# Rebuilding the attention slot of a two-layer encoder kernel: transposes move into the score banks, and ScalarE alone empties them

## Chip, cores and metric

One Trainium2 chip, one core. The metric is the device time in microseconds of one execution of the whole program, which is one launch. Smaller is better.

## What is computed

One inference step of a two-layer streaming encoder, in float32, for 1024 prompt frames and 64 sample frames (1088 columns in all, `TOK`), with 256 cached frames for the sample stream. Each layer is

```python
x = x + rmsnorm(mixer(rmsnorm(x)))
x = x + rmsnorm(squared_relu_mlp(rmsnorm(x)))
```

The mixer of layer 0 has two kinds of heads, and layer 1 has a third:

```python
# kind A, 4 heads with two maps each (differential attention, chunk-causal, ALiBi)
w = softmax(s0 + bias) - lam * softmax(s1 + bias);  oa = rmsnorm(w @ v)
# kind B, 8 heads: softmax(s + decay) @ v, causal, decay = cum_q - cum_k
# kind C, 16 heads: softmax(s + table[clip(q - k)]) @ v over the own chunk and 8 chunks before
```

Queries, keys and values come from one product of the normed input with `w_in`, and new keys and values are outputs too.

## The kernel before

**Layout.** Everything is kept feature-major: 128 features on the partitions, the 1088 columns along the free axis, in the chunks 384, 384 and 320 (`CHUNKS`). Float32 products are made as three f32r products (high x high, low x high, high x low), so one 128x128 weight tile times one chunk is three matmuls, and one *step* (one chunk of one of Q, K and V, 8 weight tiles) is 24 matmuls, called products here (`product`, L1175, the matmul at L1180). Weights arrive as units of 128x1024: SyncE loads one into `WS`, ScalarE casts it to `WH` (`hi_unit`, L647, L653), GpSimd subtracts for `WL` (`lo_unit`, L519, L522).

**Attention groups.** 16 groups of 128 features, each with two heads (or the two maps of kind A), run one after the other: 4 of kind A, 4 of B, 8 of C. While the attention of group g runs, TensorE also makes the Q, K and V of group g+1 in 9 steps (216 products), which keep it busy between the attention matmuls. The last group of each layer has no such products (`proj=False`, "alone" below). An iteration is one group; it is a hardware loop on every engine (`runs`, L370).

**Slots.** An iteration has 11 slots. The queries are taken in blocks of 128 in the order 7, 6, 5, 4, 3, 2, 1, the sample block, 0 (`ORDER`). In slot s TensorE makes the scores of block number s (`scores`, L1223: Q high/low times K high/low, 6 matmuls for each head and bank, heads side by side on the two halves of the array). VectorE adds the bias and takes the maximum (`scores`, L981, the operation at L988, which writes `PR`, and L993), ScalarE takes the exponential (`exps`, L748, L752), VectorE divides by the sum (`sums`, L1024, L1032, or the combination at L1038 for kind A). Then the probabilities are transposed on TensorE (L1271) 128 columns at a time, copied out of PSUM to `PT`, and multiplied with the transposed values `V` (L1286, L1290) to give the output of the block, which VectorE copies to `OT` (L1016); for kind A it is normed first and transposed back (L1019 to L1058, L1274, L740). Kind B and C have two heads to transpose, kind A one combined map. A block has up to 1024 keys in kinds A and B and up to 640 in C.

**PSUM.** 8 banks of 512 columns. Banks 0 and 1 hold the products in turn, 2 to 5 the scores (two for each head), 6 and 7 everything else. `bank_uses` (L77) lists what passes through banks 6 and 7 in an iteration: values, transposes in pieces of up to four tiles, the output, the output's transpose. The pieces take the two banks in turn, and each waits until the piece two before it is emptied (`use_bank`, L1251, semaphores `xA` and `xD`). Pieces are emptied by ScalarE and VectorE in turn, in practice one engine for each bank (`empty`, L732 and L1003).

**Order by hand.** Slots 0 to 7 have one step of products each, the ninth step is spread over slots 8 to 10 (`SLOT_PRODUCTS`). `S_AT` says after how many products of a slot the scores come (24, that is all of them, in slot 0; 0 from slot 3 on), `T_AT` where the transposes of the block before come. The output of a block follows at the end of the slot in which it is transposed.

**Between iterations.** At the top of an iteration ScalarE casts `Qh` and `Kh` (L769, L771) once all 9 steps are emptied, VectorE subtracts for `Ql` and `Kl` (L1062, L1064), and `scores(0)` on TensorE waits for `qklo`. SyncE loads the bias tables for the group at the top of its iteration, and stores K, V and the output.

Of the kernel before, what the change touches and what calls it, by code (L numbers as in the profile page):

```python
# [20 lines left out]
P = 128  # L21
D_MODEL, D_FF = 1024, 4096
KT_D = D_MODEL // P
# [11 lines left out]
S_AT = {k: [24, 8, 4, 0, 0, 0, 0, 0, 0] for k in "ABC"}  # L35
S_AT["alone"] = [0] + [12] * 8

T_AT = {k: [(12, 22)] * 8 + [(2, 6), (9, 13), (14, 24)] for k in "ABC"}
T_AT["alone"] = [(1, 11)] * 11

SLOT_PRODUCTS = [(0, 3 * KT_D)] * 8 + [(0, 6), (6, 14), (14, 3 * KT_D)]
# [26 lines left out]


class Use:  # L70


    def __init__(self, what, block, m, tiles, engine):
        self.what, self.block, self.m, self.tiles, self.engine = what, block, m, tiles, engine


def bank_uses(kind):  # L77

    slots = [[] for _ in range(11)]
    for n, t in enumerate(([0, 1, 2], [3, 4, 5, 6], [7, SAMPLE + 2])):  # L80
        slots[0].append(Use("V", None, 0, t, "AD"[n % 2]))
    for s in range(1, 11):
        ot = [Use("OT", ORDER[s - 2], 0, [], "A")] if s >= 2 and kind == "A" else []
        if s == 10:
            slots[s] += ot
        else:
            b = ORDER[s - 1]
            tiles = key_tiles(kind, b)
            n = 0
            for m in range(1 if kind == "A" else 2):  # L90
                for o in range(0, len(tiles), 4):
                    slots[s].append(Use("T", b, m, tiles[o:o + 4], "AD"[n % 2]))
                    n += 1
            slots[s] += ot + [Use("PV", b, 0, tiles, "D")]
    flat = [u for slot in slots for u in slot]
    count = {"A": 0, "D": 0}
    for n, u in enumerate(flat):
        u.n = n
        count[u.engine] += 1
        u.nth = count[u.engine]  # L100
        u.bank = n % 2
        u.prev = flat[n - 2] if n >= 2 else None
    return slots, flat, count


USES = {k: bank_uses(k) for k in "ABC"}
# [45 lines left out]
FROM_ONE = ("S", "ttr", "xpe", "xA", "xD")  # L152


def make_sections():
# [4 lines left out]
    def attention(layer, kind, g0, reps, proj):  # L160
        _, flat, count = USES[kind]
        per = dict(qkhi=2, qklo=2, S=18, ttr=18, nm=18, ex=18, ri=9, xpe=len(flat), xA=count["A"], xD=count["D"],
                   bias=16 if kind == "A" else 32, vc=16, kst=16, vst=16, evD=9 * proj)
        if kind == "A":
            per.update(cs=9, comb=9, ms=9, rs=9, on2=9)
        else:
            per.update(sc=18)
# [93 lines left out]
def build_program(nc, x_in, w_in, gains_in, subg_in, bf_in, lam_in, kcache, vcache, logf_cache, alibi, rel_bias,  # L261
# [4 lines left out]
    with ctx:  # L266
# [54 lines left out]
        ON, a = place("ON", a, [P, P])  # L321
# [21 lines left out]
        def semaphore(name):  # L343
# [7 lines left out]
                 "xpe xA xD "  # L351
                 "ms rs on2 "
# [43 lines left out]
        def transposed(use, bank):  # L396

            rows = [P if use.what == "V" and t != SAMPLE + 2 else N_SAMPLE if use.what == "V" else t[1] for t in use.tiles]
            first = use.tiles[0] if use.what == "V" else use.tiles[0][0] // P
            buf = V[:, :, :] if use.what == "V" else PT[:, use.m, :, :]  # L400
            full = sum(n == P for n in rows)
            out = []
            if full:
                out.append((buf[:, first:first + full, :].rearrange("p t q -> p (t q)"), bank[:, 0:full * P]))
            if full < len(rows):
                last = use.tiles[-1] if use.what == "V" else first + full
                out.append((buf[0:N_SAMPLE, last, :], bank[0:N_SAMPLE, full * P:(full + 1) * P]))
            return out


        @block.sync
        def _(sp):
# [9 lines left out]

# [14 lines left out]
            for sec in SECTIONS:  # L437
# [16 lines left out]
                elif sec.kind == "ATT":  # L454
                    if sec.g0 % GROUPS == 0:
                        norms_over(sp, sec)
                        sp.wait_ge(sem["toep"], 16)
# [1003 lines left out]
```

## Time and profile before

| | |
|---|---|
| median of 3 runs | 3188.15 us (3185.65 to 3194.68) |
| profiled execution, own time | 3186.88 us |
| its span, first to last instruction | 3185.1 us |
| TensorE busy in the span | 2909.5 us (91%) |
| VectorE, ScalarE, GpSimd busy | 1473.7, 841.5, 660.7 us |
| mean granted TensorE clock | 0.954 of full speed |
| one iteration with products, kinds A, B, C | about 75.4, 79.0, 71.8 us |
| the two groups alone, last product before to first product after | 78.1 and 75.1 us |

A row of the trace with the line L1180 is a product. "Idle before" is what an engine stood still just before an instruction, with what ended it. Matmuls are pipelined: the time from one start to the next is what a matmul costs, the duration behind it is longer.

### The profile page before, as it was taken

The page shows a single profiled execution, that of the slowest core. Times are in us where ns is not written, and L with a number is a line of the kernel's source. Part 1 is how long each engine was busy: PE and PEld are TensorE (multiplying, and loading weights), DVE is VectorE, ACT ScalarE, POOL GpSimd, SP SyncE. Part 2 cuts the span into 40 slices and gives each one's busy share as a digit, 9 for nine tenths or more (in the row PEclk, how much of TensorE's full clock was granted, in tenths as well). Part 3 has the DMA queues.
Part 4 walks back from the last instruction along what each step waited for, and adds up shares of the span by engine and source line. Part 5 has one row for each costly group of instructions (what it writes and reads, how often), then busy time and mean ns, then how long its engine had stood idle before and what let it go on. Part 6 is the DMA issues. An engine that isn't in the chain of part 4 may idle for free.

```text
span 3185.1 us, 50566 instructions
## 1 busy us (share of the span) xinstructions
PE 2909.5 (91%) x18736; PEld 2751.3 (86%) x18736; DVE 1473.7 (46%) x3593; ACT 841.5 (26%) x1621; POOL 660.7 (21%) x442
## 2 busy tenths in 40 slices
PE   5888899969899999999988998997799999999996
PEld 5777777748899999999987777776789999999996
DVE  4566655550833333333385566555255333333334
ACT  3333333342411111111233333333342110111111
POOL 1111110023321221221331010001341221221223
PEclk8999989979999999999989999998899999999998
DMA  4211111132210110110221122111221101101102
GB/s 157 78 53 52 52 64 63 63 109 92 83 53 28 53 52 27 53 53 28 73 113 48 54 87 74 54 54 67 98 93 44 54 33 46 53 33 46 53 34 113
DMA packets 52589, 201.93 MB, mean 63 GB/s; under 512 B 6728, under 2 KB 10960, under 8 KB 49024
## 3 DMA queue, kind: packets, MB, share of 16 engines
q1 hardware_dynamic: 48608, 160.56, 14.2%
q0 software_dynamic: 3888, 40.11, 3.1%
q8 instruction: 61, 1.00, 0.1%
q14 instruction: 32, 0.26, 0.0%
HBM read 154.97 MB, written 51.97 MB: 65 GB/s over the span
## 4 chain that ended last, share of the span: by engine, by line
PE 78%; DVE 9%; issue 7%; ACT 2%; DMA 2%; POOL 1%; DVEq 0%; SPq 0%; ACTq 0%; POOLq 0%
PE ps L1180 66%; PE ps L1271 3%; PE ps L1290 3%; DVE PR L1032 2%; PE ps L1286 1%; PE ps L1235 1%; DVE PR L988 1%; DVE XL L889 1%; DVE DG L871 1%; DVE ACC L879 1%; PE ps L1245 1%; ACT PR L752 1%; PE ps L1247 1%; DMA BIAS<-nc_scr 1%; PE ps L1167 0%
## 5 line engine op out<-in xcount | busy, mean ns | idle before, releaser
L1180 PE MATMUL ps<-XH,WH 128*128 128x384 f32 (+1 forms) x3096 | 1064.0, 344 | 62.9 <-DVE XL L889 22.4
L1180 PE MATMUL ps<-XH,WL 128*128 128x384 f32 (+1 forms) x3096 | 1045.6, 338 | 0.0
L1180 PE MATMUL ps<-XL,WH 128*128 128x384 f32 (+1 forms) x3096 | 1035.9, 335 | 0.0
L522 POOL TENSOR_TENSOR WL<-WS,WH 128x1024 fp32r<-128x1024 f32 x193 | 464.8, 2409 | 1843.2 <-ACT WH L653 1843.1
L1180 PE MATMUL ps<-U,WH 128*128 128x384 f32 (+1 forms) x3072 | 757.6, 330 | 0.0
L1180 PEld LDWEIGHTS ps<-XH,WH 128*128 128x128 f32 x3096 | 599.3, 194 | 94.3 <-issue 80.0
L1180 PEld LDWEIGHTS ps<-XH,WL 128*128 128x128 f32 x3096 | 597.8, 193 | 7.9 <-issue 6.2
L1180 PEld LDWEIGHTS ps<-XL,WH 128*128 128x128 f32 x3096 | 599.1, 194 | 4.3 <-issue 3.1
L1180 PEld LDWEIGHTS ps<-U,WH 128*128 128x128 f32 x3072 | 547.0, 189 | 0.0
L1180 PE MATMUL ps<-U,WL 128*128 128x384 f32 (+1 forms) x1536 | 506.8, 330 | 0.0
L653 ACT CAST WH<-WS 128x1024 fp32r<-128x1024 f32 x193 | 201.2, 1043 | 685.1 <-PE ps L1180 662.6
L1130 DVE TENSOR_TENSOR ACC<-ps,ACC 128x384 f32<-128x384 f32 (+1 forms) x336 | 178.2, 535 | 429.9 <-PE ps L1180 429.9
L752 ACT ACTIVATE PR<-PR,NM 128x640 f32<-128x640 f32 (+8 forms) x288 | 206.6, 717 | 572.0 <-DVE NM L993 570.8
L1110 DVE SCALAR_TENSOR_TENSOR TU<-ps,RB 128x384 f32<-128x384 f32 (+1 forms) x192 | 102.8, 536 | 408.1 <-PE ps L1180 408.1
L1180 PEld LDWEIGHTS ps<-U,WL 128*128 128x128 f32 x1536 | 290.1, 189 | 0.0
L820 ACT ACTIVATE U<-TU 128x384 fp32r<-128x384 f32 (+1 forms) x192 | 97.7, 509 | 615.5 <-DVE TU L1110 615.5
L1271 PE MATMUL ps<-ident,PR 128*128 128x128 f32 (+1 forms) x996 | 181.3, 293 | 84.0 <-DVE PR L1032 56.6
L1271 PEld LDWEIGHTS ps<-ident,PR 128*128 128x128 f32 (+1 forms) x996 | 126.6, 148 | 113.6 <-issue 54.3
L988 DVE CUSTOM_DVE_ANT_0 PR<-ps,BIAS 128x640 f32<-128x640 f32 (+8 forms) x288 | 196.1, 681 | 12.6 <-issue 11.3
L1290 PE MATMUL ps<-PT,V 128*64 128x128 f32 (+1 forms) x1680 | 129.8, 298 | 14.1 <-DVE PT L1008 13.8
L1290 PEld LDWEIGHTS ps<-PT,V 128*64 128x64 f32 (+1 forms) x1680 | 97.6, 147 | 45.6 <-issue 36.4
L1032 DVE TENSOR_SCALAR PR<-PR,RI 128x640 f32<-128x640 f32 (+8 forms) x216 | 135.0, 667 | 3.8
(111 smaller groups left out, 2162.7 us busy)
## 6 DMA issues: line engine op xcount, KB each, us to landing
WS<-w_in SPq DMA_DIRECT2D x193, 512.0 KB, 4.4
k_out<-KT SPq DMA_DIRECT2D x16, 672.0 KB, 5.1
x_scr<-XRES POOLq DMA_DIRECT2D x6, 1536.0 KB, 5.5
XRES<-x_scr POOLq DMA_DIRECT2D x6, 1536.0 KB, 6.7
v_out<-VT SPq DMA_DIRECT2D x16, 544.0 KB, 5.8
o_scr<-OT SPq DMA_DIRECT2D x14, 544.0 KB, 2.9
XRES<-x_in POOLq DMA_DIRECT2D x4, 1536.0 KB, 9.2
BIAS<-nc_scr SPq DMA_DIRECT2D x8, 672.0 KB, 6.1
```

The costliest lines, as they stand in the source:

```text
L522: pool.tensor_tensor(WL[u][:, :], WS[STAGE[u]][:, :], WH[u][:, :].bitcast(f32), ALU.subtract)\
L653: act.copy(WH[u][:, :], WS[st][:, :]).then_inc(sem["whi"], 1)
L752: act.activation(PR[:, s % 2, m, 0:n], PR[:, s % 2, m, 0:n], ACT.Exp, bias=NM[:, q:q + 1], accum_out=L[:, q:q + 1]).then_inc(sem["ex"], 1)
L820: act.activation(ct(U, c, u), TU[:, t % 2, 0:w], ACT.Square).then_inc(sem["uhi"], 1)
L871: ins = dve.tensor_scalar(DG[0:v, j % 2, q * P:q * P + v], ident[0:v, 0:v], RS[0:v, q:q + 1], None, ALU.mult)
L988: dve.tensor_tensor_reduce(out=PR[:, s % 2, m, 0:n].rearrange("p (b w) -> p b w", b=nb), in0=ps[:, 2 + 2 * m:2 + 2 * m + nb, 0:n // nb], i ...
L1032: dve.tensor_scalar(PR[:, s % 2, m, 0:n], PR[:, s % 2, m, 0:n], RI[:, q + m:q + m + 1], None, ALU.mult)\
L1110: dve.scalar_tensor_tensor(out=TU[:, t % 2, 0:w], in0=ps[:, t % 6, 0:w], scalar=0.0, in1=RB[:, o:o + w], op0=ALU.max, op1=ALU.mult).then_i ...
L1130: dve.tensor_tensor(acc, ps[:, v % 6, 0:w], acc, ALU.add).then_inc(sem["evD"], 1)
L1180: return pe.matmul(bank[:, 0:w], wt, xt, start=m == 0, stop=m == 3 * tiles - 1, skip_group_check=False)
L1271: ins = pe.transpose(bank[0:v, n * P:(n + 1) * P], PR[:, st, use.m, o:o + v], ident[:, :])
L1290: ins = pe.matmul(bank[f, 0:P], V[0:v, t, f], PT[0:v, m, o // P, :], **ends)
```

## The change

The two-bank traffic of `bank_uses` is gone. The transposes of a block go to banks 2 to 5, the same that its successor's scores have just left, all tiles of both heads in one piece (up to 8 tiles, two banks, for each head). ScalarE empties them with one copy of up to 1024 columns for each head. In slot s TensorE now does: the scores of block s, the output of block s-2 (bank 6), products, the transposes of block s-1 (after VectorE has read the scores of block s, and 11/20 of the slot's products), products. The scores of block s+1 wait until ScalarE has emptied the transposes (`emptied`). The ninth step goes to bank 7. Products are shared out by a table (`SLOT_END`) in proportion to the block; slots 9 and 10 have 20 and 22 (22 and 22 in C). The scores of block 0 come after 5 products, not 24. `Qh` and `Kh` are made in slots 9 and 10 of the iteration before, each as soon as its last step is emptied; `Ql` and `Kl` too. GpSimd makes the second and third low unit only after `Kl`. SyncE's loop is written out, and the bias tables of the next group are loaded at the end of the iteration before.

```diff
-SLOT_PRODUCTS = [(0, 3 * KT_D)] * 8 + [(0, 6), (6, 14), (14, 3 * KT_D)]
+SLOT_END = {"A": [26, 52, 76, 96, 114, 130, 144, 158, 174, 194, 216],
+            "B": [26, 52, 76, 96, 114, 130, 144, 158, 174, 194, 216],
+            "C": [24, 46, 64, 82, 100, 118, 136, 154, 172, 194, 216]}
+S_AT = [5] + [0] * 8
...
+    return p0, p0 + (14 if s == 0 else (p1 - p0) * 11 // 20), p1
...
-        ON, a = place("ON", a, [P, P])
+        ON, a = place("ON", a, [P, 2, P])
...
+        def both(m):
+
+            return ps[:, 2 + 2 * m:4 + 2 * m, :].rearrange("p b w -> p (b w)")
...
+                            after = (sec, i + 1) if i + 1 < sec.reps else (SECTIONS[SECTIONS.index(sec) + 1], 0)
+                            bias(*after)
+                            values(*after)
...
+                            pool.wait_ge(sem["qklo"], sec.at(i, "qklo", 4))
+                            lo_unit(sec, i, 1, 1)
+                            lo_unit(sec, i, 2, 2)
...
+                        def empty_turned(k):
+                            act.wait_ge(sem["T"], sec.at(i, "T", k + 2))
+                            for m in range(1 if kind == "A" else 2):
+                                for dst, src in turned(kind, k, m):
+                                    ins = act.copy(dst, src)
+                            ins.then_inc(sem["tA"], 1)
...
+                                if s == 9:
+
+                                    act.wait_ge(sem["S"], sec.at(i, "S", 18))
+                                    act.wait_ge(sem["evD"], sec.at(i, "evD", 7))
+                                    act.copy(Qh[:, 0:TOK], QT[:, :]).then_inc(sem["qkhi"], 1)
+                                if s == 10:
+                                    act.wait_ge(sem["evD"], sec.at(i, "evD", 8))
+                                    act.wait_ge(sem["kc"], sec.at(i, "kc", 16))
+                                    act.copy(Kh[:, :], KT[:, :]).then_inc(sem["qkhi"], 1)
...
+                        if sec.proj:
+                            hi_unit(sec, i, 2, 2, 1, sec.at(i, "D", 9))
...
+                            if sec.proj and s == 9:
+                                low_queries(sec.at(i, "qkhi", 3))
+                            if sec.proj and s == 10:
+                                low_keys(sec.at(i, "qkhi", 4))
+                            if kind == "A" and s >= 2:
+                                normed(s - 2)
+                            if sec.proj:
+                                for t in steps_in(kind, s):
+                                    empty_dense(t)
...
+                        def emptied(k):
+
+                            wait(pe, "tA", sec.at(i, "tA", k))
+                            wait(pe, "tD", sec.at(i, "tD", min(k, 1)))
...
                             wait(pe, "ttr", sec.at(i, "ttr", 2 * s))
+                            emptied(s)
...
+                        def turn(k):
+
+                            if k < 8:
+                                pe.wait_ge(sem["ttr"], sec.at(i, "ttr", 2 * (k + 2)))
...
+                                pe.wait_ge(sem["sc"], sec.at(i, "sc", 2 * k + 2))
...
+                            for p in range(p0, p1 + 1):
+                                if s < 9 and p == p0 + (S_AT[s] if sec.proj else 0):
                                     scores(s)
-                                for use in uses:
-                                    if at[use] == m:
-                                        use_bank(use, s)
...
+                                if s >= 2 and p == p0:
+                                    outputs(s - 2)
+                                if p == turn_at:
+                                    if kind == "A" and s >= 3:
+                                        turn_output(s - 3)
+                                    if s == 0:
+                                        turn_values()
+                                    elif s < 10:
+                                        turn(s - 1)
```

**ScalarE, the end of an iteration of kind C (from the weight cast of the seventh step).** Names: `WH_51` to `WH_53` are the three high weight units. Before:

```order
L653 CAST WH_52<-WS_60 128x1024 [waits s_D]
L751 REGISTER_ALU
L752 ACTIVATE PR,L<-PR,NM 128x128 [waits s_nm]
L734 REGISTER_ALU
L745 COPY PT<-ps 128x256 [waits s_xpe]
L745 COPY PT<-ps 64x128
L751 REGISTER_ALU
L752 ACTIVATE PR,L<-PR,NM 128x128 [waits s_nm]
L734 REGISTER_ALU
L745 COPY PT<-ps 128x128 [waits s_xpe]
L367 REGISTER_ALU [waits s_ld2]
L653 CAST WH_53<-WS_61 128x1024 [waits s_D]
```

Changed:

```order
L739 COPY PT<-ps 128x128
L643 REGISTER_ALU
L339 REGISTER_ALU [waits s_ld1]
L645 CAST WH_52<-WS_60 128x1024 [waits s_D]
L783 REGISTER_ALU
L784 REGISTER_ALU [waits s_S]
L785 CAST Qh<-QT 128x1088 [waits s_evD]
L787 REGISTER_ALU
L788 REGISTER_ALU [waits s_evD]
L789 CAST Kh<-KT 128x1344 [waits s_kc]
L339 REGISTER_ALU [waits s_ld2]
L645 CAST WH_53<-WS_61 128x1024 [waits s_D]
```

The casts of the queries and keys have moved in front of the third weight cast, behind the second; the second weight cast now waits for the eighth step (slot 9) right before them.

**VectorE, slots 9 and 10 of an iteration of kind C, changed.** (Before, slots 9 and 10 hold two copies of `PT`, two of `OT` and the last step's `VT`; `Ql` and `Kl` open the next iteration.)

```order
L1011 COPY OT<-ps 128x64 [waits s_pv]
L975 REGISTER_ALU
L976 TENSOR_TENSOR Ql<-QT,Qh 128x1088 [waits s_qkhi]
L1044 REGISTER_ALU
L909 TENSOR_TENSOR KT<-ps,RB 128x256 [waits s_kst,s_qkhi,s_D]
L910 TENSOR_TENSOR KT<-ps,RB 128x64
L1005 REGISTER_ALU
L1011 COPY OT<-ps 128x128 [waits s_pv]
L979 REGISTER_ALU
L980 TENSOR_TENSOR Kl<-KT,Kh 128x1344 [waits s_qkhi]
L1044 REGISTER_ALU
L913 TENSOR_TENSOR VT<-ps,RB 128x320 [waits s_T,s_vst,s_D]
```

The last third of the keys (`KT`, the eighth step) is emptied behind `Ql`, and `Kl` stands behind that.

**ScalarE, slot 2 of kind C.** Before:

```order
L752 ACTIVATE PR,L<-PR,NM 128x640 [waits s_nm]
L734 REGISTER_ALU
L745 COPY PT<-ps 128x512 [waits s_xpe]
L751 REGISTER_ALU
L752 ACTIVATE PR,L<-PR,NM 128x640 [waits s_nm]
L734 REGISTER_ALU
L745 COPY PT<-ps 128x512 [waits s_xpe]
```

Changed:

```order
L732 ACTIVATE PR,L<-PR,NM 128x640 [waits s_nm]
L731 REGISTER_ALU
L732 ACTIVATE PR,L<-PR,NM 128x640 [waits s_nm]
L736 REGISTER_ALU
L739 COPY PT<-ps 128x640 [waits s_T]
L739 COPY PT<-ps 128x640
```

VectorE's copies of the fifth tile of each head (128x128, L1008) are gone with this.

## Rows read from the trace of the kernel before

**Rows 1.** Busy time by stretch: one iteration each of kind A, B, C (instructions; then clock share)

```profile
261.60:337.00 75.40, 66.56 (x429) 59.07 (x429) 46.80 (x152) 28.26 (x65) 12.29 (x12) 0.95 0.15 55
492.00:571.00 79.00, 71.91 (x572) 61.08 (x572) 46.63 (x135) 26.90 (x58) 7.16 (x3) 0.95 0.18 63
1905.20:1977.00 71.80, 65.64 (x503) 56.34 (x502) 42.96 (x139) 25.83 (x59) 7.22 (x3) 0.98 0.16 60
```

**Rows 2.** TensorE in order of time, one iteration of kind C: the longest wait and the last

```profile
1918.93 0.65 PE L1271 MATMUL ps<-ident,PR 128*128 128x128 f32 x4 [1.73 <-ACT PT L745]
...
1976.70 0.44 PE L1180 MATMUL ps<-XH,WH 128*128 128x384 f32 x1 [0.66 <-DVE VT L915]
```

**Rows 3.** The same view: products of 384 columns, then of 320

```profile
1924.55 0.33 PE L1180 MATMUL ps<-XH,WH 128*128 128x384 f32 x1
1924.72 0.33 PE L1180 MATMUL ps<-XL,WH 128*128 128x384 f32 x1
...
1975.44 0.31 PE L1180 MATMUL ps<-XH,WH 128*128 128x320 f32 x1
1975.58 0.31 PE L1180 MATMUL ps<-XL,WH 128*128 128x320 f32 x1
```

**Rows 4.** Groups by line and shape, VectorE (busy us, mean ns, idle before)

```profile
L988 DVE CUSTOM_DVE_ANT_0 PR<-ps,BIAS 128x640 f32<-128x640 f32 x80 | 65.8, 822 | 2.9 <-issue 2.2
...
L1062 DVE TENSOR_TENSOR Ql<-QT,Qh 128x1088 fp32r<-128x1088 f32 x16 | 36.0, 2248 | 34.8 <-ACT Qh L769 34.8
...
L1064 DVE TENSOR_TENSOR Kl<-KT,Kh 128x1344 fp32r<-128x1344 f32 x16 | 24.8, 1549 | 0.0
...
L988 DVE CUSTOM_DVE_ANT_0 PR<-ps,BIAS 128x1024 f32<-128x1024 f32 x16 | 19.6, 1222 | 8.3 <-issue 8.3
...
L911 DVE TENSOR_TENSOR KT<-ps,RB 128x256 f32<-128x256 f32 x16 | 6.6, 413 | 4.6 <-PE ps L1180 4.6
...
L912 DVE TENSOR_TENSOR KT<-ps,RB 128x64 f32<-128x64 f32 x16 | 3.3, 209 | 0.0
```

**Rows 5.** Groups by line and shape, ScalarE

```profile
L653 ACT CAST WH<-WS 128x1024 fp32r<-128x1024 f32 x193 | 201.2, 1043 | 685.1 <-PE ps L1180 662.6 <-DMA WS<-w_in 22.3
...
L745 ACT COPY PT<-ps 128x512 f32<-128x512 f32 x128 | 74.3, 581 | 25.9 <-PE ps L1271 22.3
...
L771 ACT CAST Kh<-KT 128x1344 fp32r<-128x1344 f32 x16 | 21.0, 1311 | 0.0
...
L769 ACT CAST Qh<-QT 128x1088 fp32r<-128x1088 f32 x16 | 17.6, 1099 | 0.0
...
L745 ACT COPY PT<-ps 128x256 f32<-128x256 f32 x32 | 11.3, 354 | 0.7 <-PE ps L1271 0.5
```

**Rows 6.** In order of time: `Ql` with GpSimd still (first), and beside its `WL`

```profile
112.24 1.29 DVE L1062 TENSOR_TENSOR Ql<-QT,Qh 128x1088 fp32r<-128x1088 f32 x1 [4.82 <-ACT Qh L769]
...
1977.20 2.41 POOL L522 TENSOR_TENSOR WL<-WS,WH 128x1024 fp32r<-128x1024 f32 x1 [9.66 <-ACT WH L653]
...
1978.16 2.60 DVE L1062 TENSOR_TENSOR Ql<-QT,Qh 128x1088 fp32r<-128x1088 f32 x1 [1.59 <-ACT Qh L769]
```

**Rows 7.** TensorE in order of time, the groups alone of kind B and C

```profile
650.07 0.31 PE L1180 MATMUL ps<-XH,WL 128*128 128x320 f32 x1
656.65 0.80 PE L1235 MATMUL ps<-Kh,Qh 64*128 64x512 f32 x2 [6.27 <-DVE Kl L1064]
...
2209.00 0.64 PE L1235 MATMUL ps<-Kh,Qh 64*128 64x320 f32 x2
...
2215.00 0.74 PE L1271 MATMUL ps<-ident,PR 128*128 128x128 f32 x5 [1.85 <-DVE PR L1032]
...
2217.55 0.63 PE L1235 MATMUL ps<-Kh,Qh 64*128 64x320 f32 x2
```

**Rows 8.** Busy time by stretch: alone groups, last product before to first after

```profile
650.40:728.54 78.14, 43.98 (x355) 32.54 (x356) 38.97 (x126) 36.28 (x81) 27.02 (x26) 0.73 0.33 114
2191.50:2266.60 75.10, 43.04 (x285) 32.27 (x285) 35.44 (x130) 35.22 (x81) 26.88 (x26) 0.66 0.32 113
```

More of the change, by code:

```diff
@@ L67, in key_tiles @@
     return [(o, min(P, n - o), first + o // P) for o in range(0, n, P)]
[L70 to L106, printed above, removed]
 class Section:
@@ L394, in norms_over, with turned, queries @@
             wait(eng, "fst", 48)
[L396 to L401, printed above, removed]
+        def both(m):
+            return ps[:, 2 + 2 * m:4 + 2 * m, :].rearrange("p b w -> p (b w)")
+        def turned(kind, k, m):
+            tiles = key_tiles(kind, ORDER[k])
+            full = sum(v == P for _, v, _ in tiles)
             out = []
             if full:
[L404 to L407, printed above, removed]
-            return out
+                out.append((PT[:, m, 0:full, :].rearrange("p t q -> p (t q)"), both(m)[:, 0:full * P]))
+            if full < len(tiles):
+                out.append((PT[0:N_SAMPLE, m, full, :], both(m)[0:N_SAMPLE, full * P:(full + 1) * P]))
+            return out
+        def queries(kind, k):
+            q0 = block_of(kind, ORDER[k])[0]
+            return slice(q0, q0 + (N_SAMPLE if ORDER[k] == SAMPLE else P))
         @block.sync
@@ L454, in _, with bias @@
                 elif sec.kind == "ATT":
-                    if sec.g0 % GROUPS == 0:
+                    first = sec.g0 % GROUPS == 0
+                    if first:
                         norms_over(sp, sec)
                         sp.wait_ge(sem["toep"], 16)
-                    with runs(sp, sec) as i:
-                        g = sec.pick(i, sec.g0, 1)
+                    def bias(sec, i):
+                        g = sec.g0 + i
                         wait(sp, "ttr", sec.at(i, "ttr"))
@@ L726, in _ @@
                     kind = sec.att
-                    pace = kind if sec.proj else "alone"
                     if sec.g0 % GROUPS == 0:
@@ L785, in _ @@
[L785 to L787 removed]
+                            if s < 9:
                                 exps(s, 0)
                                 exps(s, 1)
[L790 to L795 removed]
@@ L993, in scores @@
                             dve.tensor_scalar(NM[:, q:q + 1], M[:, q:q + 1], -1.0, None, ALU.mult).then_inc(sem["nm"], 1)
-                        def set_free(s):
-                            if s < 2:
-                                wait(dve, "xpe", sec.at(i, "xpe"))
-                            else:
-                                last = [use for use in USES[kind][1] if use.what == "T" and use.block == ORDER[s - 2]][-1]
-                                dve.wait_ge(sem["xpe"], sec.at(i, "xpe", last.n + 1))
@@ L1217, in _ @@
                     kind = sec.att
-                    pace = kind if sec.proj else "alone"
                     if sec.g0 % GROUPS == 0:
```

334 lines of the change are left out of this document (155 added, 179 removed).

## Prediction

> **What bounds the kernel now.** I read the windows first. TensorE is busy 91% of the span (the table above), so time can only come out of TensorE's idle stretches and out of stretches at the lower clock. In one iteration with products it is idle 75.40 - 66.56 = 8.8 us in kind A, 79.00 - 71.91 = 7.1 us in B and 71.80 - 65.64 = 6.2 us in C, and the granted clock is 0.95, 0.95 and 0.98 [rows 1]. The 14 such iterations hold 4x8.8 + 3x7.1 + 7x6.2 = 100 us of idle time. The two groups alone take 78.1 and 75.1 us, with TensorE busy 44 and 43 of them, at a clock of 0.73 and 0.66 [rows 8]. The rest of the program, MLP and output products, is not touched.
>
> Then the order of time: where the idle time ends tells what it waited for. In an iteration of C the longest wait, 1.73 us, is a transpose that waits for its bank to be emptied, behind a late first block; the last one is 0.66 us at the start of the next iteration, which waits for the ninth step to be emptied [rows 2]. The groups alone start 6.27 us after the last product, for `Kl` [rows 7]. Products follow each other every 0.17 us (384 columns) or 0.147 us (320) [rows 3]; that is the full clock, 2.4 GHz.
>
> **The work on TensorE stays.** Products, scores, transposes and outputs are the same in number and shape, so the busy time of rows 1 stays and the question is what idle time remains.
>
> **ScalarE alone empties.** A copy of 256 columns takes 0.354 us, one of 512 takes 0.581 [rows 5], so 0.89 ns a column: 640 columns 0.69, 1024 columns 1.04. Two heads are 1.4 us in C and up to 2.1 in B, one map up to 1.04 in A. This lies between the transposes and the scores of the next slot, and TensorE covers it with the products of the second part of a slot: C, slots 2 to 8, 9 products, 9 x 0.17 = 1.55 plus 0.1 for the change of kind, against 1.4 plus 0.1 of hand-over; B, slot 1, 12 products, 2.2 against 2.1. The exponentials of the slot are over by then: they end about 4.4 us into a slot of C, the transposes at 5.2. So it costs nothing, by a margin of 0.1 to 0.2 us. If that cover fails, TensorE stands before every scores block. Bounds: 0 and, if each copy came late by its hand-over, 0.15 us a slot, 8 x 14 x 0.15 = 17 us. I take 3 us, since slot 3 of B (9 products against two copies of 768) just misses.
>
> The PSUM page of the Trainium skill ("PSUM — Partial Sum Buffer", specifications) says that ScalarE and VectorE may read PSUM at the same time, each at full bandwidth, as long as they are in different banks. By that rule this change gives away half of the emptying speed, 0.7 us a slot in C. No row here shows both at one block's banks at once. With the cover above the sum would be the same either way.
>
> **VectorE before the transposes.** A transpose now overwrites scores, so it waits for VectorE's pass: 1.22 us a head for 1024 columns, 0.82 for 640 [rows 4], with its small operations about 1.34 and 1.03 from one to the next. From slot 2 on, the output block and about ten products (3 us) cover the two passes. In slot 0 only nine products, 1.6 us, stand against 3.0 us (A, B) or 2.2 us (C): TensorE idles **1.4 us** in A and B and **0.5 us** in C. In slot 1 of A and B 14 products (2.5) stand against 2.7: 0.2. In A, slots 5 to 8 also wait for the copy of the output before they transpose the one before: 0.8 in all.
>
> **The border between iterations.** The casts and subtractions for the next group now start inside this one, as a chain: eighth step's last product drained 0.3, then the weight cast `WH` 1.04 that stands in front on ScalarE, `Qh` 1.10, `Ql`, the keys emptied 0.41 + 0.21, `Kh` 1.31, `Kl` 1.55 [rows 4, 5]. `Ql` takes 1.29 us with GpSimd still, and 2.60 beside its `WL` [rows 6]; the low units are moved behind `Kl`, so I take 1.29. Sum 7.2, with six hand-overs of 0.05, 7.5 us. TensorE has in that time 24 products x 0.147 = 3.5, an output block of one tile 0.35, and 5 products of the next iteration 0.9: 4.75. So it idles **2.8 us** before `scores(0)` in B and C. In A the chain also holds two small norm operations on VectorE (0.35 each, an estimate from the copies of that width), and TensorE stands already at the last output's transpose, before the iteration's end: 8.2 - 4.0 = **4.2 us**. Moved past on SyncE: bias and `V` loads come before the output's store; both have over 5 us of slack, as has the store.
>
> **Sum for an iteration.** A: 4.2 + 1.4 + 0.2 + 0.8, with 0.5 of small gaps, 7.1 instead of 8.8: -1.7. B: 2.8 + 1.4 + 0.3 + 0.5 = 5.0 instead of 7.1: -2.1, less 0.2 for the slots that just miss: -1.9. C: 2.8 + 0.5, with gaps and misses 1.2, 4.5 instead of 6.2: -1.7. Together 4 x 1.7 + 3 x 1.9 + 7 x 1.7 = **-24 us**. I leave the clock as it is: its half-speed stretch sits at the end of the iteration now, where slots 8 to 10 are thin; that thinness goes, and a stall of 2.8 to 4.2 us takes its place.
>
> **First iteration of each layer.** `scores(0)` comes after 5 products, not 24, and meets `Kl`, which is not ready: 2.2 us in layer 0, 0.7 in layer 1: **+3 us**.
>
> **The groups alone.** Their start moves from 6.3 us behind the last product to about 3.7 (7.5 less 24 products and an output): -2.7 each. A slot of C alone takes 2217.55 - 2209.00 = 8.55 us; its transposes at 2215.00 waited 1.85 us for exponentials and division [rows 7]. The change transposes the block before, so the loop is scores 1.9 (half clock), the passes 2.1, ten transposes 2.1, copies 1.4, hand-overs 0.3: 7.8. -0.75 over nine slots is -7 each. Bounds for the two groups: nothing, and -30. I take 2 x (2.7 + 7) = **-20 us**.
>
> **Sum:** -24 + 3 - 20 = -41 us against the profiled execution's 3186.9, 3146; the median of the runs shown is 1.3 above it, so 3147.
>
> **Rivals.**
> 1. *The bank loop becomes the bound (slower).* Banks 2 to 5 now pass through scores, VectorE, transposes and ScalarE in series. In C that is 1.1 + 2.1 + 1.1 + 1.4 + 0.3 = 6.0 us of a slot of 6.7. For: ScalarE's part is not halved, and the margin behind the transposes is 0.1. Against: both parts of the loop fit as counted. It decides the sign if it costs over 41/112 = 0.37 us in each of the 112 slots; at 0.55 us it is +62: 3208.
> 2. *The clock.* The stall at the border is the longest that an iteration has, and if the lower level (1.2 GHz) follows each, 14 times some 2 us are lost: 3147 + 28 = 3175. For: after 6.27 us of idle the groups alone run at 0.66 to 0.73 [rows 8]. Against: after the 1.73 us wait C keeps 0.98. The page "TensorE: Matmul & The Clock Gate" of the Trainium skill (part 1) says that an idle array falls back to half rate, and gives A's 4.2 us more reason than C's 2.8.
> 3. *The border chain is hidden better, or the alone groups gain more:* 3122. For: 100 us of idle time is there to take; the alone groups are half idle.
> 4. *The idle time only moves:* waits now at the border and before the transposes take back all; 3187.
>
> **Chances.** Forecast 0.58, rival 1 0.08, rival 2 0.14, rival 3 0.13, rival 4 0.07. A measurement of this kernel can tell about 0.3%, 9.6 us, from no change. Forecast and rival 3 are faster, rival 2 for the most part; slower is rival 1 alone. Faster 0.83, same 0.09, slower 0.08. The range reaches from below rival 3 over rival 2: 3112 to 3182.
>
> **What would show it.** In the changed profile: iterations of about 73.7, 77.1 and 70.1 us; before `scores(0)` one idle stretch of 2.8 us put down to `Kl`, in A 4.2 us before the output's transpose; before the values' transposes 1.4 or 0.5 us put down to VectorE; no idle time over 0.2 us before scores in slots 2 to 8; `Ql` at 1.29 us; alone groups near 68 and 65 us. It is wrong if scores wait for ScalarE in every slot, if `Ql` still takes 2.6, or if the clock of an iteration falls under 0.93.

## The result and the profile after

The changed kernel takes 3068.86 us (median of 4 runs, 3067.46 to 3073.83) against 3191.41 for the kernel before in the same comparison: ratio 0.962, 95% interval 0.9598 to 0.9641. That is 122.6 us less by the medians and 119.3 by the spans of the two profiled executions (3065.8 against 3185.1), where the forecast had 41. The direction was right, the size three times too small, and the time lies below the range.

The head of the page after (busy time, share of the span, instructions):

```profile
span 3065.8 us, 49510 instructions
...
PE 2851.0 (93%) x18736; PEld 2726.9 (89%) x18736; DVE 1354.9 (44%) x3409; ACT 893.0 (29%) x1677; POOL 659.6 (22%) x442
```

TensorE executes the same 18,736 matmuls, is busy 93% of the span and not 91%. The page hides where. Busy time by stretch, one iteration of kinds A, B and C, then the two groups alone (length, busy time of TensorE, its weight loads, VectorE, ScalarE, GpSimd, with instructions; then the share of the clock granted, the DMA share and GB/s); they answer to [rows 1] and [rows 8]:

```profile
248.50:316.67 68.17, 62.73 (x430) 56.28 (x430) 43.12 (x148) 30.80 (x64) 12.02 (x13) 1.00 0.17 61
454.20:525.80 71.60, 69.56 (x573) 60.88 (x572) 35.73 (x122) 31.52 (x63) 7.13 (x3) 0.98 0.20 70
1821.92:1886.88 64.96, 62.68 (x503) 55.97 (x502) 33.56 (x126) 29.06 (x63) 7.13 (x3) 1.00 0.18 66
597.42:667.88 70.46, 39.61 (x356) 30.52 (x356) 32.79 (x112) 38.64 (x85) 29.41 (x27) 0.77 0.32 112
2081.80:2145.70 63.90, 34.01 (x286) 26.07 (x286) 31.69 (x116) 35.96 (x85) 29.33 (x27) 0.75 0.34 123
```

Cut at the same products in both traces, the whole difference is this:

| stretch | before, us | after, us | difference | forecast |
|---|---|---|---|---|
| 4 iterations A | 302.3 | 276.5 | -25.9 | -6.8 + 2.2 |
| 3 iterations B | 237.8 | 212.6 | -25.2 | -5.7 |
| 7 iterations C | 504.4 | 455.3 | -49.1 | -11.9 + 0.7 |
| 2 groups alone | 153.7 | 134.4 | -19.3 | -20 |
| all else | 1986.9 | 1987.1 | +0.2 | 0 |

So the groups alone came as forecast in their sum, and the miss of 79 us is in the iterations with products. These have lost 100.1 us, and the traces divide it in two parts. TensorE's idle time in the 14 went from 97.2 to 41.4 us: -55.8 (forecast -21 net of the first iterations). Its busy time went from 947.2 to 902.9: -44.3 (forecast: stays). Of the busy time, the clock explains most: an iteration of A had 0.95 and has 1.00, one of C had 0.98 and has 1.00. The time lost to the lower of the two levels (1.2 GHz) is at most (1 - share) of a stretch; summed over the 14 iterations that was 44.4 us before and is 11.1 now, so the clock gave back up to 33 us. Comparing the interval between like neighbouring matmuls at both levels, which leaves out half-speed time that fell into waits, gives 34 before and 9 after, some **26 us** (an estimate from the two traces). I had put that at nothing. The other 18 us of busy time are what the first experiment is about.

Before, six waits of TensorE of over 0.3 us make up 6.0 of the 6.2 us of idle time in an iteration of C: 0.66 at the border, 0.44, 1.73 ([rows 2]), 0.37, and these two in the thin slots at its end, in the trace of the kernel before:

```profile
1967.79 0.55 PE L1271 MATMUL ps<-ident,PR 128*128 128x128 f32 x3 [1.55 <-DVE PR L1032]
1969.87 1.28 PE L1290 MATMUL ps<-PT,V 128*64 128x128 f32 x12 [1.25 <-DVE PT L1008]
```

What idle time is left in the changed kernel (TensorE in order of time; in brackets the idle time before and what ended it). First kind A, then the border of a B iteration, then one of C:

```profile
312.41 0.30 PE L1296 MATMUL ps<-ident,ON 128*128 128x128 f32 x1 [2.20 <-DVE ON L1019]
...
316.11 0.33 PE L1296 MATMUL ps<-ident,ON 128*128 128x128 f32 x1 [1.94 <-DVE ON L1058]
...
254.07 1.09 PE L1256 MATMUL ps<-ident,VT 128*128 128x128 f32 x8 [1.07 <-DVE M L997]
...
457.23 0.50 PE L1236 MATMUL ps<-Kh,Qh 64*128 64x512 f32 x2 [1.98 <-DVE Kl L980]
...
1889.90 0.42 PE L1236 MATMUL ps<-Kh,Qh 64*128 64x320 f32 x2 [1.99 <-DVE Kl L980]
...
1893.11 1.09 PE L1256 MATMUL ps<-ident,VT 128*128 128x128 f32 x8 [0.30 <-DVE M L997]
```

A has 2.20 + 1.94 us before the last two outputs' transposes and 1.07 before the values'; B 1.98 before `scores(0)`; C 1.99 there and 0.30 before the values'. Nothing else of over 0.3 us is in an iteration after the first of its layer: from 1893.1 to the next border TensorE of C has no gap. The border's chain in C, on ScalarE and then on VectorE:

```profile
1881.83 0.43 ACT L739 COPY PT<-ps 128x128 f32<-128x128 f32 x2 [2.54 <-PE ps L1271]
1883.00 1.05 ACT L645 CAST WH<-WS 128x1024 fp32r<-128x1024 f32 x1 [0.73 <-PE ps L1175]
1883.95 1.09 ACT L785 CAST Qh<-QT 128x1088 fp32r<-128x1088 f32 x1
1886.94 1.31 ACT L789 CAST Kh<-KT 128x1344 fp32r<-128x1344 f32 x1 [1.90 <-DVE KT L910]
...
1885.08 1.29 DVE L976 TENSOR_TENSOR Ql<-QT,Qh 128x1088 fp32r<-128x1088 f32 x1 [5.18 <-ACT Qh L785]
1886.29 0.42 DVE L909 TENSOR_TENSOR KT<-ps,RB 128x256 f32<-128x256 f32 x1
1886.62 0.21 DVE L910 TENSOR_TENSOR KT<-ps,RB 128x64 f32<-128x64 f32 x1
...
1888.29 1.56 DVE L980 TENSOR_TENSOR Kl<-KT,Kh 128x1344 fp32r<-128x1344 f32 x1 [1.26 <-ACT Kh L789]
```

It is the chain of the forecast, link by link: `WH` (L645), `Qh` (L785), `Ql` (L976, 1.29 us, GpSimd being still), the keys emptied (L909, L910), `Kh` (L789), `Kl` (L980).

### The profile page after: what moved, and what is told of

The parts are those of the page before. It is cut to its first block, busy times and chain, and to the rows that moved or that the text cites. A ratio compares the mean times of both kernels' runs of the same rounds, so it can differ in the third digit from the quotient of the medians.

```text
span 3065.8 us, 49510 instructions
## 1 busy us (share of the span) xinstructions
PE 2851.0 (93%) x18736; PEld 2726.9 (89%) x18736; DVE 1354.9 (44%) x3409; ACT 893.0 (29%) x1677; POOL 659.6 (22%) x442
## 4 chain that ended last, share of the span: by engine, by line
PE 83%; issue 5%; DVE 4%; ACT 2%; POOL 1%; DMA 1%; DVEq 0%; SPq 0%; ACTq 0%; POOLq 0%
PE ps L1175 69%; PE ps L1271 4%; PE ps L1289 3%; PE ps L1236 2%; PE ps L1285 1%; PE ps L1246 1%; PE ps L1248 1%; DVE DG L869 1%; DVE ACC L877 1%; ACT Kh L789 1%; DVE PR L997 1%; PE ps L1162 1%; DVE XL L887 1%; ACT Qh L785 1%; PE ps L1256 0%
## 5 line engine op out<-in xcount | busy, mean ns | idle before, releaser
L1175 PE MATMUL ps<-XH,WH 128*128 128x384 f32 (+1 forms) x3096 | 1033.2, 334 | 56.3 <-DVE XL L887 22.1
L1175 PE MATMUL ps<-XH,WL 128*128 128x384 f32 (+1 forms) x3096 | 1030.4, 333 | 0.0
L1175 PEld LDWEIGHTS ps<-XH,WH 128*128 128x128 f32 x3096 | 592.0, 191 | 62.8 <-issue 50.9
L1175 PEld LDWEIGHTS ps<-XL,WH 128*128 128x128 f32 x3096 | 591.7, 191 | 11.1 <-issue 11.1
L1175 PEld LDWEIGHTS ps<-XH,WL 128*128 128x128 f32 x3096 | 591.2, 191 | 9.1 <-issue 9.1
L645 ACT CAST WH<-WS 128x1024 fp32r<-128x1024 f32 x193 | 201.4, 1044 | 652.2 <-PE ps L1175 625.1
L739 ACT COPY PT<-ps 128x384 f32<-128x384 f32 (+4 forms) x280 | 137.3, 541 | 144.6 <-PE ps L1271 144.0
L1271 PE MATMUL ps<-ident,PR 128*128 128x128 f32 (+1 forms) x996 | 137.3, 279 | 8.7 <-DVE M L997 8.5
L1236 PE MATMUL ps<-Kh,Qh 64*128 64x320 f32 (+5 forms) x416 | 85.2, 403 | 52.4 <-DVE Kl L980 23.6
L1271 PEld LDWEIGHTS ps<-ident,PR 128*128 128x128 f32 (+1 forms) x996 | 117.1, 143 | 18.2 <-DVE M L997 12.8
L1289 PE MATMUL ps<-PT,V 128*64 128x128 f32 (+1 forms) x1680 | 120.9, 285 | 3.3 <-ACT PT L739 3.1
```

The lines of the kernel that those rows point to most:

```text
L645: act.copy(WH[u][:, :], WS[st][:, :]).then_inc(sem["whi"], 1)
L739: ins = act.copy(dst, src)
L1175: return pe.matmul(bank[:, 0:w], wt, xt, start=m == 0, stop=m == 3 * tiles - 1, skip_group_check=False)
L1236: pe.matmul(out[m][:, 0:w], Qh[half[m], q], Kh[half[m], k], start=True, stop=False)
L1271: ins = pe.transpose(both(m)[0:v, n * P:(n + 1) * P], PR[:, k % 2, m, o:o + v], ident[:, :])
L1289: ins = pe.matmul(ps[f, 6, 0:P], V[0:v, t, f], PT[0:v, m, o // P, :], **ends)
```

## The experiments

Seven kernels, each the changed kernel with an edit. Medians are of 4 or 5 runs, against 3068.9 for the changed kernel. The kernel before took 3191.1 us beside `split`, `both_engines` and `early_qh`, and 3194.4 beside the other four, so totals of the two batches compare to about 3 us; the stretches come from one trace of each kernel. "C" is the iteration of kind C, 64.97 us in the changed kernel.

### split: TensorE comes back to the transposes more often

The transposes of a block (one call before) go in parts of three, one product between them, the last part where the whole block was.

```diff
-                            for m in range(1 if kind == "A" else 2):
-                                for n, (o, v, _) in enumerate(key_tiles(kind, ORDER[k])):
-                                    ins = pe.transpose(both(m)[0:v, n * P:(n + 1) * P], PR[:, k % 2, m, o:o + v], ident[:, :])
-                            ins.then_inc(sem["T"], 1)
+                            parts = turn_parts(k)
+                            for m, n, o, v in parts[part]:
+                                ins = pe.transpose(both(m)[0:v, n * P:(n + 1) * P], PR[:, k % 2, m, o:o + v], ident[:, :])
+                            if part == len(parts) - 1:
+                                ins.then_inc(sem["T"], 1)
...
+                                    for part in range(late + 1):
+                                        if p == turn_at - (late - part) * sec.proj:
+                                            turn(s - 1, part)
```

> The changed kernel with the transposes of a block in parts of three with one product between them (up to four visits of TensorE to the transposes instead of one, some 17 more in an iteration of kind C), the last part where the whole block was. Theory 'a visit costs': between the kernels an iteration of C has 20 visits less and, beside idle time and half clock, 1.5 us less busy time, 0.08 us a visit; then 17 visits more cost 1.3 to 1.5 us an iteration, 14 iterations some 20 us, 3089. Rival 'visits are free, busy time fell for the clock alone': 3067 to 3072. A third case, that ScalarE's margin of 0.1 us before the scores breaks as well, shows as idle time before scores.

Measured 3081.18 us, +12.3. Two iterations of C by stretch, one at the full clock and one with time at the lower level:

```profile
1702.92:1768.52 65.60, 63.07 (x503) 55.80 (x502) 33.56 (x126) 29.06 (x63) 7.14 (x3) 1.00 0.19 65
1768.52:1835.21 66.69, 64.43 (x504) 57.38 (x502) 33.56 (x126) 29.06 (x63) 7.13 (x3) 0.97 0.18 64
```

The waits of TensorE in the second (us in total, times, longest):

```profile
PE ps L1236 <- DVE Kl L980: 2.0, 1, 2.0
PE ps L1277 <- DVE M L997: 0.3, 1, 0.3
```

At the full clock C is 0.63 us longer, 0.25 of it idle (the first part now comes before VectorE's pass is over, L1277). TensorE turns back to products 38 times in it, against 21 in the changed kernel and 41 in the one before (counted in the traces), so 17 more visits cost 0.38 us, **0.02 us each**, not 0.08. With the idle time counted in, it is 0.04. Both theories miss: visits are not free, but the 20 saved ones are worth 0.4 to 0.7 us of the 6.8 that C gained. The rest of the +12.3 is for the most part the clock (0.97 in two of the six later iterations of C, under 1.00 in the last three of A), which no theory of this run had in it, and in B 0.8 us an iteration of waiting at L1277.

### both_engines: VectorE empties the second head

Kinds B and C; the order is otherwise the same.

```diff
-                            for m in range(1 if kind == "A" else 2):
-                                for dst, src in turned(kind, k, m):
-                                    ins = act.copy(dst, src)
+                            for dst, src in turned(kind, k, 0):
+                                ins = act.copy(dst, src)
...
+                        def empty_turned(k):
+                            dve.wait_ge(sem["T"], sec.at(i, "T", k + 2))
+                            for dst, src in turned(kind, k, 1):
+                                ins = dve.tensor_copy(dst, src)
+                            ins.then_inc(sem["tD"], 1)
...
                             if s < 9:
                                 sums(s)
+                            if kind != "A" and 1 <= s <= 9:
+                                empty_turned(s - 1)
```

> The changed kernel, kinds B and C, with VectorE emptying the second head's transposes and ScalarE the first's, all else as it is. Theory 'ScalarE's copies are covered, who empties does not matter': iterations of C stay at 64.97 us, of B at 71.6; the groups alone, where copies stand on the chain, gain up to 0.7 us a slot: 3058 to 3070. Rival 'one engine for both heads is where the gain is' (VectorE's copies stand in front of its passes and emptied steps): C iterations 1 to 3 us longer, 3080 to 3110. Rival 'half the emptying speed was given away': iterations shorter by over 1 us, under 3055.

Measured 3072.76 us, +3.9, not clear of noise (ratio to the kernel before 0.9626, 0.9609 to 0.9643, against 0.9598 to 0.9641). C, to be held against the third row of the stretches above (1821.92 to 1886.88):

```profile
1824.17:1889.07 64.90, 62.62 (x503) 55.92 (x502) 39.10 (x136) 25.04 (x53) 7.14 (x3) 1.00 0.18 66
```

VectorE has 5.5 us more work in an iteration and ScalarE 4.0 less, and TensorE's time is the same to 0.1 us; B gains 0.2 to 0.5. The groups alone lose 2.7 and 3.6 us, where I expected a gain; in the first it is 2.1 us more idle time of TensorE, in the second 3.3 us more busy time at a clock of 0.72 instead of 0.75. So in the iterations it does not matter which engine empties: that ScalarE does it alone is worth nothing there. The 100 us come from the rest of the change, which this kernel shares. How they divide among the move into the score banks, the sharing out of the products and the earlier casts was not tried.

One thing more is in this trace. The code of kind A is the same in both kernels, and so are the waits of its second iteration (1.08, 2.20 and 1.94 us), yet that one ran at 0.98 here and at 1.00 in the changed kernel. The clock of a single iteration is no sure consequence of its waits.

### copy_two: ScalarE's copies cost double

```diff
+                                ins.then_inc(sem["dup"], 1)
+                                act.wait_ge(sem["dup"], sec.at(i, "dup", k + 1 if kind == "A" else 2 * k + m + 1))
+                                for dst, src in pieces:
+                                    ins = act.copy(dst, src)
```

> The changed kernel with ScalarE's copies of each head's transposes out of PSUM done twice, one after the other. Theory 'the cover is thin': in the trace of the changed kernel the copies end 0.17 to 0.6 us ahead of the next scores in C, 0.05 to 0.27 in B, 0.55 to 1.0 in A. Doubled they take 1.4 us more a slot in the wide blocks of C, up to 2.1 in B: C +5.8 us an iteration, B +8.5, A +0.5, groups alone +9 each, together +86, 3155, all of it as idle time of TensorE before scores. Rival 'TensorE's queue has more slack than that': under +30, 3100.

Measured 3204.09 us: +135, ratio to the kernel before 1.0041 (1.0027 to 1.0055), all gain gone. An iteration of C and one of B by stretch:

```profile
1832.65:1905.53 72.88, 63.29 (x503) 56.01 (x502) 33.56 (x126) 39.05 (x83) 7.14 (x3) 1.00 0.16 59
471.62:553.95 82.33, 70.16 (x574) 60.86 (x573) 35.72 (x122) 42.80 (x83) 7.12 (x3) 0.98 0.17 61
```

The waits of TensorE in the one of C:

```profile
PE ps L1241 <- ACT PT L744: 6.3, 7, 1.3
PE ps L1241 <- DVE Kl L985: 2.0, 1, 2.0
```

ScalarE does 10.0 us more in C and TensorE stands 7.3 us more for ScalarE, 6.3 of them in seven waits before scores (L1241), the eighth before an output. B +10.7 to +12.6, the groups alone +20.0 and +13.8, A +0.8 to +2.2. So the cover is thin, as the forecast said: 1.4 us more of copies in a wide slot of C gave a wait of up to 1.26. Rival 1 (the bank loop becomes the bound) is what happens when it is gone. The size was 86 expected, 135 measured: the groups alone lost 34 us and not 18, the second copy also waits for the first, and the clock fell in some iterations. A second reading: at the full clock, eight waits more cost an iteration of C 7.29 us idle and 7.83 in all, so each wait costs 0.07 us of busy time beside its idle time.

### late_casts: the border's chain after the iteration

`Qh`, `Kh`, `Ql`, `Kl` are made after the ninth step and its `WH`.

```diff
                         if sec.proj:
                             hi_unit(sec, i, 2, 2, 1, sec.at(i, "D", 9))
+                            act.wait_ge(sem["S"], sec.at(i, "S", 18))
+                            act.wait_ge(sem["evD"], sec.at(i, "evD", 8))
+                            act.copy(Qh[:, 0:TOK], QT[:, :]).then_inc(sem["qkhi"], 1)
+                            act.wait_ge(sem["kc"], sec.at(i, "kc", 16))
+                            act.copy(Kh[:, :], KT[:, :]).then_inc(sem["qkhi"], 1)
...
+                        if sec.proj:
+                            low_queries(sec.at(i, "qkhi", 3))
+                            low_keys(sec.at(i, "qkhi", 4))
```

> The changed kernel with Qh, Kh, Ql and Kl made after the ninth step and its weight cast, at the end of the iteration's own lists. Chain from the last product: drained 0.3, WH 1.04, Qh 1.1, Kh 1.31, Kl 1.56, hand-overs 0.2, and 1 more if Ql runs beside GpSimd's WL: 5.5 to 6.5 us, against 0.9 of products: TensorE idle 4.6 to 5.6 before scores(0), C and B +2.5 to +3.5, A +1 (its output transposes no longer wait). Theory 'the clock follows these waits, and the change got its clock back by making them few': the clock of an iteration of C falls from 1.00 to 0.95 to 0.976 in each, 1.4 to 2.7 us more: 3068 + 36 + 20 to 30 = 3125 to 3135. Rival 'the clock has to do with something else in the kernel before': clock stays at 1.00 in C, 3100 to 3108.

Measured 3092.18 us, +23.3. Two iterations of C by stretch:

```profile
1837.79:1905.88 68.09, 64.02 (x504) 57.53 (x503) 33.75 (x125) 29.07 (x63) 7.12 (x3) 0.97 0.19 63
1905.88:1974.46 68.58, 64.51 (x504) 57.93 (x503) 33.77 (x125) 29.06 (x63) 7.10 (x3) 0.95 0.18 63
```

The only wait of TensorE in the second:

```profile
PE ps L1231 <- DVE Kl L976: 4.1, 1, 4.1
```

The wait grew to 4.1 us, less than the 4.6 to 5.6 expected (`Ql` runs beside `Kh` and with GpSimd still, 1.29 us, so it adds nothing), and the clock fell in every one of the six later iterations of C, to 0.95 or 0.975. C is 3.1 us longer, 1.8 of it idle, 1.3 clock. B, with waits of 4.1 to 4.3 us, had 0.95 in all three. So the clock follows a wait of this length, and the rival's 1.00 in C is refuted. The total misses both theories' numbers because the wait was smaller, the clock cost the low end of 1.4 to 2.7, and A, which changes its waits for this one, rose by 0.6 to 0.7 only and fell by 5.1 in its first iteration.

### scores_first: a border wait of 2.9 us

```diff
-S_AT = [5] + [0] * 8
+S_AT = [0] + [0] * 8
```

> The changed kernel with the first scores of an iteration at product 0, not 5: the wait at the border is 0.85 us longer in B and C (2.9 instead of 2.0), A's is the outputs' and stays. Theory 'a wait of this length in an otherwise gapless iteration is at the edge of what costs clock': C shows the lower clock in more than none of its iterations, each 1.4 us; with +0.8 us each for the wait: 3075 to 3090. Rival 'only the sum of several waits costs clock': C stays at 1.00, +8 at most: 3070 to 3077.

Measured 3081.91 us, +13.0. Two iterations of C by stretch, one before the clock began to fall and one after:

```profile
1700.45:1765.68 65.23, 62.38 (x503) 55.98 (x502) 33.57 (x125) 29.07 (x63) 7.15 (x4) 1.00 0.18 66
1833.34:1901.57 68.23, 65.38 (x503) 58.85 (x501) 33.57 (x125) 29.06 (x63) 7.09 (x4) 0.95 0.18 63
```

The only wait in the latter:

```profile
PE ps L1236 <- DVE Kl L980: 2.9, 1, 2.9
```

At the full clock the iteration is 0.26 us longer, with 0.57 more idle time and 0.31 less busy time; where the clock is 0.95 it is 3.3 us longer. It fell below 1.00 in five of the six later iterations, as the first theory has it. So with a border wait of 2.0 us C keeps 1.00 in six of six later iterations of the changed kernel (six of six in `both_engines`, four of six in `split`), with 2.9 us in one of six, with 4.1 in none, and the kernel before, with waits of 1.55, 1.25 and 0.66 us within 10 us (the last of them in [rows 2]), had 0.976 or less in all. A longer wait makes the lower level likelier, then, but length alone does not settle it. B, with the same 1.98 us, is at 0.98 in both of its later iterations in the changed kernel, and in one of two in `split` and in `both_engines`. A has 2.20 and 1.94 us, 1.5 us apart, and the full clock in three of four. The iterations of C in one trace are close copies of each other, so six of six is less than six independent cases.

### early_qh: the chain starts with the eighth step

```diff
+                            if sec.proj and s == 9:
+                                act.wait_ge(sem["S"], sec.at(i, "S", 18))
+                                act.wait_ge(sem["evD"], sec.at(i, "evD", 7))
+                                act.copy(Qh[:, 0:TOK], QT[:, :]).then_inc(sem["qkhi"], 1)
                             if 1 <= s <= 9:
                                 empty_turned(s - 1)
...
-                                if s == 9:
...
-                                    act.copy(Qh[:, 0:TOK], QT[:, :]).then_inc(sem["qkhi"], 1)
```

> The changed kernel with the cast of Qh on ScalarE ahead of the eighth block's copy and the weight cast, where the queries have long been emptied; so Ql too. Theory 'the stall at the border is a chain that starts at the eighth step': the chain loses WH, Qh and Ql, is keys emptied, Kh, Kl, some 4 us against 4.9 of TensorE's work: no idle before scores(0), C -2.1 us, B -2.1 and its half-clock stretch, A -2 to -4: 3035 to 3042. Rival 'the next wait takes its place' (weights, the last output, VectorE's passes before the values' transposes, which then have less cover): only -10 to -15, 3055.

Measured 3040.61 us, -28.2, ratio to the kernel before 0.9527 (0.9511 to 0.9543). An iteration of C by stretch:

```profile
1808.21:1871.05 62.84, 62.57 (x504) 55.91 (x503) 35.16 (x125) 29.07 (x63) 7.14 (x3) 1.00 0.19 68
```

The waits of TensorE, first its only one in that iteration, then the two longest of an iteration of A:

```profile
PE ps L1256 <- DVE M L997: 0.3, 1, 0.3
...
PE ps L1296 <- DVE ON L1058: 1.9, 1, 1.9
PE ps L1256 <- DVE M L997: 0.9, 1, 0.9
```

C is 62.84 us: the wait for `Kl` is gone and 2.13 us with it, 2.0 of it idle and 0.1 at the restart. Nothing took its place in C: the stall at the border is this chain. B is 2.3 us shorter, but there the next wait did take half of its place. An iteration of B by stretch, and its only wait:

```profile
451.51:520.77 69.26, 68.13 (x573) 59.63 (x572) 37.15 (x121) 31.52 (x63) 7.15 (x3) 1.00 0.20 73
...
PE ps L1256 <- DVE M L997: 1.1, 1, 1.1
```

Its idle time fell by 0.9 us only (2.04 to 1.13), and the other 1.4 are busy time, with the clock at 1.00 and not 0.98. A gained only 0.3 to 1.0: its idle time fell by 2.0 to 2.7, but one wait of 1.9 remains, for the last scaling of an output that stands behind `Kl` on VectorE (L1058), and the clock went to 0.975 in all three, though they wait less than before. So the total lies in the first theory's range partly by luck: A gave 3.7 us in all where 8 to 16 were expected, and the groups alone gave 7.3 that no theory had.

### early_all: two more edits

In A the ninth output's scaling goes ahead of `Kl` on VectorE, and the values' transposes move from product 14 to 20 (A, B) or 15 (C).

```diff
-    return p0, p0 + (14 if s == 0 else (p1 - p0) * 11 // 20), p1
+    return p0, p0 + ((15 if kind == "C" else 20) if s == 0 else (p1 - p0) * 11 // 20), p1
...
+                            if kind == "A" and s == 10:
+                                normed(8)
                             if sec.proj and s == 10:
                                 low_keys(sec.at(i, "qkhi", 4))
```

> Three edits on the changed kernel: Qh ahead of the eighth block's copy and weight cast (as in early_qh), the ninth output's last scaling ahead of Kl on VectorE in kind A, and the values' transposes at product 20 (A, B) or 15 (C), not 14. Against early_qh, whose trace shows 1.93 us idle before A's last output transpose and 0.9 to 1.08 before the values' transposes in A and B: A -1.5 - 0.9 - its half-clock stretch 1.4, B -1.0, C 0: -15 - 3 = 3022 to 3027. Rival 'the values are emptied too late for the next scores': VectorE and ScalarE empty them 0.5 us before scores(1) are due, and A and B give the 1 us back: 3030 to 3034.

Measured 3021.30 us (5 runs, 3019.11 to 3023.46), ratio to the kernel before 0.9462 (0.9448 to 0.9475), 0.7 us under what the first theory has, and the fastest of all. Iterations of A, B and C by stretch:

```profile
240.72:304.38 63.66, 62.67 (x432) 56.19 (x430) 43.12 (x148) 30.69 (x64) 12.03 (x12) 1.00 0.18 65
437.01:505.19 68.18, 68.10 (x573) 59.61 (x572) 37.14 (x121) 31.53 (x63) 7.15 (x3) 1.00 0.21 74
1790.91:1853.57 62.66, 62.56 (x503) 55.91 (x502) 35.10 (x125) 29.07 (x63) 7.15 (x3) 1.00 0.19 69
```

A is 63.66 us, 4.5 less than in the changed kernel, B 68.18, C 62.66, all three at the full clock; idle time in the 14 iterations is 6.5 us, 2.0 of it in the first.

## Why the prediction was wrong

**Right.** What bounds the kernel, and that the idle time of the iterations is the store to draw on. The chain at the border: its links, its place, that it is put down to `Kl` in B and C and before the last outputs' transposes in A, shown by `early_qh` and `late_casts`. Its size in A, 4.2 forecast, 2.20 + 1.94 measured, though in two waits and not one. `Ql` at 1.29 us. The groups alone: 70.5 and 63.9 us against "near 68 and 65", together -19.3 against -20. Here two misses cancel: the start came 3.3 us sooner in each, not 2.7, and the rest gave 4.5 and 8.2 us, not 7 each. ScalarE's copies cost nothing, by a thin cover, and the sign turns if that cover goes (`copy_two`). And the sentence that faster emptying would not change the sum: `both_engines` halves ScalarE's part and gains nothing. The page "PSUM — Partial Sum Buffer" of the Trainium skill (specifications), that the two engines read PSUM in parallel at full bandwidth, agrees with this trace: ScalarE's copy of 640 columns takes 0.69 us beside VectorE's (from 1844.76 and 1844.84) and 0.70 in the changed kernel. With the copies covered it is worth nothing.

**Wrong, first step: "I leave the clock as it is", some 26 us.** The forecast had the half-speed stretches of [rows 1] in hand (0.95, 0.95, 0.98) and named the thin end of the iteration as their place, then said that a border wait takes its place. `scores_first` and `late_casts` show that its size counts: one wait of 2.0 us in an iteration otherwise almost without them kept 2.4 GHz in most iterations of C, one of 2.9 in one of six, one of 4.1 in none. In B 2.0 us did not keep it in the changed kernel, and those two iterations at 0.98 are part of the 9 us still lost. That the several waits at the old iteration's end were what held the clock down fits this, but they were not put back by themselves; what decides for a wait of 2 us stays open. Rival 2 had the right mechanism with the wrong sign; it took the groups alone, which start with 6.27 us of waiting ([rows 7], [rows 8]), as the nearest case. The page "TensorE: Matmul & The Clock Gate" of the Trainium skill (part 1) says that an idle array falls back to half rate; this holds after all waits of 4.1 us in `late_casts`, and after 2.0 us in B but not in C of the changed kernel.

**Wrong, second step: the idle time that remains, 35 us.** The forecast left 7.1, 5.0 and 4.5 us in A, B and C; measured in the later iterations 5.4, 2.0 and 2.3 (1.1 in the first of B). Term by term, for C: border 2.8, measured 1.99, since casts start before the one in front has ended and the chain is 7.2 us from where the forecast starts it, not 7.5, against 5.2 of cover, not 4.75; values 0.5, measured 0.30; "gaps and misses" 1.2, measured none. For B: border 2.8, measured 1.98; the values' 1.4, measured 1.06 in the iteration with the full clock and none in the other two, where TensorE at the lower clock after the border comes late enough; misses of 0.8, measured none. For A: border 4.14 as forecast, values 1.07 for 1.4, slots 5 to 8 nothing for 0.8. The small terms stand in a place that comes back 14 times: "gaps", "misses" and "slots 5 to 8", for none of which a row stood, make some 16 of the 35 us.

**Wrong, third step: "the busy time of rows 1 stays", 18 us beside the clock's.** The number and shape of the matmuls stayed, not the way they lie: 20 returns to products less in an iteration of B or C, at 0.02 to 0.04 us (`split`), and in C four waits less, at 0.07 us each (`copy_two`; 0.12 in `early_qh`), together 0.7 to 1.2 us. C's ledger is then 3.9 idle, 1.4 clock and these, 6.0 to 6.5 of 6.84; what makes up the rest is open.

**First iterations.** Layer 0: 71.98 us against 68.17 for the next one, where before it was 76.18 against 75.42, so +3.1 beside the forecast's 2.2. Layer 1: 65.48 against 64.97, where before it was 73.64 against 72.50; the 0.7 did not come. The waits for `Kl` there measured 1.61 and 0.21 us.

## What to carry to other kernels

A tuned kernel's short waits are paid up to three times: idle, at the restart behind them, and, in some iterations, by the clock; when an edit gathers many waits into one, price all three, and take the clock share from the rows of the very stretch that the edit clears. Count a term that repeats in every slot only if a row shows it, and sum the ends of the range from the same repeated terms. And ask of a change with a name what else it moves: here "ScalarE alone empties" was worth nothing in the iterations, and what came with it 100 us.

## What the runs showed of the hardware

- The granted clock answers to waits of 2 to 4 us in an otherwise busy TensorE: in later iterations of C with a border wait of 2.0 us it was 1.00 in 16 of 18 (changed kernel, `both_engines`, `split`), of 2.9 us in 1 of 6, of 4.1 us in 0 of 6; in B with 2.0 us in 2 of 6. A fall to 0.975 costs 1.3 to 1.4 us an iteration; one to 0.95 about 3 in `scores_first`, and 1.8 in `late_casts`, where part of it lay in the wait.
- Less waiting is not always more clock: A has 1.00 in three of four iterations of the changed kernel with 2.20 and 1.94 us, and 0.975 in its three later ones in `early_qh` with 1.9 and 0.4 to 1.1.
- In `split` the same wait of 2.0 us, at the same place of the program, lowers the clock in one iteration (1768.52, 0.97) and not in the one before it (1702.92, 1.00). Why was not tried.
- A turn to another kind of matmul and back costs 0.02 to 0.04 us (`split`), a restart after a wait 0.07 to 0.12 us (`copy_two`, `early_qh`).
- Both engines read PSUM side by side without slowing ScalarE: its copy of 640 columns took 0.69 us beside VectorE's of 0.82 from other banks (`both_engines`, 1844.76 and 1844.84), and 0.70 without it (changed kernel).
